# Seven block products for eight in a gated feed-forward block of an fp32 transformer kernel

## The reference, cut to what matters

```
D_MODEL = 1024
D_FF_2 = ((8 * D_MODEL // 3 + 255) // 256) * 256
def swiglu(h, w_gu, w_down):
    a, b = jnp.split(h @ w_gu, 2, axis=-1)
    return (jax.nn.silu(a) * b) @ w_down
...
    x = x + mx[2] * (jnp.concatenate([att_x, hg_x], axis=-1) @ w_out[l])
    x = x + mx[5] * swiglu(modulate(rmsnorm(x, g_norm2[l]), mx[3], mx[4]), w_gu[l], w_down[l])
return rmsnorm(x, g_final)
```

## Time and profile before

| | |
|---|---|
| median of 3 runs | 3163.41 us (3162.6 to 3164.22) |
| span of the profiled execution | 3166.7 us (first to last instruction; the page gives no time around it) |
| PE busy | 3023.6 us, 15087 matmuls |
| DVE busy | 1568.1 us, 1932 instructions |
| ACT busy | 1077.0 us, 1601 instructions |
| POOL busy | 634.1 us, 497 instructions |

### The profile page before, as it was taken

The page is one execution under the profiler, slowest core; times in us unless marked ns, Lnnn a source line. Parts: engine busy times, 40 slices in busy tenths (PEclk is TensorE's granted clock), DMA queues, the critical chain, the costliest instruction groups (busy, mean ns, idle before and its releaser), DMA issues.

```text
span 3166.7 us, 36928 instructions
## 1 busy us (share of the span) xinstructions
PE 3023.6 (95%) x15087; PEld 2515.2 (79%) x15087; DVE 1568.1 (50%) x1932; ACT 1077.0 (34%) x1601; POOL 634.1 (20%) x497
## 2 busy tenths in 40 slices
PE   7899999989999999999988999999999999999997
PEld 5688888878788888888866778888777888888886
DVE  7566665663465544333457874556644222232224
ACT  5555555552311212221436773223323111111111
POOL 4333333321000001000407783133300000000001
PEclk9999999999999999999999999999999999999999
DMA  3111111112234332111210001101131111111111
GB/s 125 41 47 47 47 47 48 47 67 94 67 116 123 118 114 68 47 53 48 100 35 13 11 9 56 34 27 41 47 113 40 47 53 47 47 47 47 53 41 60
DMA packets 77384, 184.80 MB, mean 58 GB/s; under 512 B 7072, under 2 KB 29088, under 8 KB 77216
## 3 DMA queue, kind: packets, MB, share of 16 engines
q1 hardware_dynamic: 77216, 182.44, 18.4%
HBM read 163.87 MB, written 15.79 MB: 57 GB/s over the span
## 4 chain that ended last, share of the span: by engine, by line
PE 84%; DVE 9%; ACT 4%; issue 2%; POOL 1%; DMA 0%; POOLq 0%; SPq 0%; DVEq 0%; ACTq 0%
PE ps L520 40%; PE ps L1638 18%; PE ps L3068 8%; DVE b L3016 2%; PE ps L2541 2%; PE ps L917 1%; DVE b L509 1%; PE ps L2348 1%; PE ps L2347 1%; PE ps L2319 1%; PE ps L924 1%; PE ps L2362 1%; ACT b L501 1%; DVE b L2411 1%; PE ps L90 1%
## 5 line engine op out<-in xcount | busy, mean ns | idle before, releaser
L520 PE MATMUL ps<-b 128*128 128x512 f32 x6012 | 1486.4, 398 | 29.7 <-DVE b L509 14.8
L520 PEld LDWEIGHTS ps<-b 128*128 128x128 f32 x6012 | 1105.7, 190 | 241.3 <-issue 20.3
L1638 PE MATMUL ps<-b 128*128 128x512 f32 x2592 | 599.1, 392 | 0.7 <-DVE b L1806 0.7
L1638 PEld LDWEIGHTS ps<-b 128*128 128x128 f32 x2592 | 485.0, 187 | 109.3 <-DVE b L1806 1.1
L509 DVE TENSOR_TENSOR b<-b 128x1024 fp32r<-128x1024 f32 (+1 forms) x206 | 255.3, 1241 | 287.2 <-ACT b L501 278.5
L501 ACT ACTIVATE b<-b 128x1024 fp32r<-128x1024 f32 (+1 forms) x206 | 214.9, 1045 | 529.3 <-PE ps L1638 427.4
L3068 PE MATMUL ps<-b 128*128 128x512 f32 (+1 forms) x1464 | 325.2, 377 | 6.3 <-ACT b L3127 5.9
L3068 PEld LDWEIGHTS ps<-b 128*128 128x128 f32 x1464 | 253.1, 190 | 55.0 <-issue 10.7
L1418 POOL TENSOR_TENSOR b<-b 128x1024 f32<-128x1024 f32 x18 | 43.1, 2397 | 910.1 <-ACT b L1449 909.6
L2390 POOL TENSOR_TENSOR b<-b 128x512 fp32r<-128x512 f32 x144 | 183.4, 1298 | 46.9 <-PE ps L2348 24.7
L1822 DVE TENSOR_TENSOR b<-b,ps 128x1024 f32<-128x1024 f32 x64 | 78.1, 1220 | 152.0 <-PE ps L1638 151.9
(11 more groups left out here) (319 smaller groups left out, 3680.9 us busy)
## 6 DMA issues: line engine op xcount, KB each, us to landing
b<-in_down SPq DMA_DIRECT2D x52, 512.0 KB, 3.6
b<-in_mod SPq DMA_DIRECT2D x96, 256.0 KB, 2.7
b<-in_gu SPq DMA_DIRECT2D x44, 512.0 KB, 3.6
b<-scratch SPq DMA_DIRECT2D x38, 512.0 KB, 4.4
b<-in_dn_in SPq DMA_DIRECT2D x32, 512.0 KB, 4.9
b<-in_up SPq DMA_DIRECT2D x32, 512.0 KB, 3.8
b<-in_win SPq DMA_DIRECT2D x26, 512.0 KB, 3.7
scratch<-b SPq DMA_DIRECT2D x18, 512.0 KB, 2.9
```

The source lines that it names most:

```text
L520: ins = e.matmul(ps[:, c], w, h[:, k, c], start=first and k == 0 and i == 0, stop=last and k == KT - 1 and i == 2)
L1638: ins = e.matmul(ps[:, c], w, u[:, at[k], c], start=k == 0 and p == 0, stop=k == n - 1 and p == 2)
```

## The change

The products of the second feed-forward block are made in Strassen's form (Winograd's variant: seven products of half-size blocks and fifteen additions). The first stage (`v` = 0 to 21) is one product of eight feature tiles in, two inner tiles out, 1024 tokens: the blocks are four feature tiles, one inner tile, 512 tokens. Even `v` is the gate of an inner pair, odd `v` the value. Each of the seven steps `i` of a `v` is 12 matmuls of 128x512 (L2985), and the weights of a step are a block or a sum of blocks:

- POOL makes the sums of weight blocks S1 to S4 (128x512), ACT rounds each of the seven (`act_wide_high`), DVE takes the remainder (`dve_wide_low`, L3061), six steps ahead of PE. Every `v` has two raw tiles of 128x1024.
- The seven activation operands `xs[0..6]` (128x4x512, high and remainder) are made once at the start, from `x2`, which is stored to DRAM first: DVE normalises (`z`, L3197), POOL forms differences (`operand`), ACT rounds, DVE takes remainders (`low`, L3206, L3208).
- ACT copies three of the partial sums out of PSUM, and `dve_wide_join` adds them to the others (L3274, L3276), silu on ACT, product on DVE (L3279, L3282). POOL forms four differences of each inner pair's blocks (`hidden`), and SP stores seven tiles of 128x512 for each pair to DRAM.

The second stage (`v` = 22 to 33, called t = 0 to 11) takes inner pairs in groups of 2, 2, 1, 2, 2, 2 (`GROUPS2`), two t for each group. SP loads the seven stored tiles of a group (`hidden` in `sp_wide`) into four buffers, ACT rounds them, DVE takes the remainder (`low_hidden`, L3162) into the seven or eight slots that are now `xs[3..6]`, and PE runs seven steps of 12 matmuls (6 for the group of one pair) with L3027. DVE adds each step's two banks to `w.x`, which was loaded again from DRAM (L3249). The end follows as before, with the last squares in halves.

The core of the diff:

```diff
-    units += mlp("gu", "down2", FF2, 6, True)
+GROUPS2 = ((0, 1), (2, 3), (10,), (4, 5), (6, 7), (8, 9))
+class Wide:
...
+        first = [(v, i) for i in range(5) for v in range(2)] + [(v, i) for v in range(2) for i in (5, 6)]
+        self.steps = first + [(v, i) for v in range(2, len(self.width)) for i in range(7)]
...
+    def t_after(self, v, i):
+        if v == self.na - 1 and i >= 3:
+            return [2 * (i - 3), 2 * (i - 3) + 1]
+        t = v - self.na
+        if t > 0 and t % 2 and 7 * (t // 2) + i + 8 < self.n_t():
+            return [7 * (t // 2) + i + 8]
+        return []
...
+    def wide_memory(self):
...
+        w.xs = [put(four + 16384 * i, [128, 4, 1024], F32R) for i in range(3)]
+        w.xs += [b[:, 4 * i:4 * i + 4, :] for b in (self.b_hi, self.b_lo) for i in range(2)]
...
+        w.ts = [put(four + 32768 + 4096 * i, [128, 2, 512]) for i in range(4)]
+        w.x = put(four, [128, KT, T])
...
+    def sp_wide(self, e, w):
...
+        def hidden(n):
...
+            if n < 4:
+                e.wait_ge(*P.at("st", w.na - 1, 2))
+            else:
+                e.wait_ge(*V.at("tlo", n - 4))
...
+            if v <= w.na and v % 2 == 0 and v:
+                store(v // 2 - 1)
+            if v + 2 < len(w.width):
+                load(v + 2)
+            if v == w.na - 1:
+                for k in range(KT):
+                    if k % 4 == 0:
+                        e.wait_ge(*P.at("st", v, k // 4))
...
+                    e.dma_start(w.x[:, k, :], self.scratch[2][:, k, :]).then_inc(*self.xl[k].up("x2"))
...
+    def pe_wide(self, e, w):
...
+                if i == 6:
+                    e.wait_ge(*V.at("q22", v))
...
+            if i in (2, 3, 4, 6):
+                e.wait_ge(*V.at("ad", t, {2: 0, 3: 1, 4: 2, 6: 4}[i]))
...
+    def dve_wide(self, e, w):
...
+            if i >= 3:
+                self.dve_wide_join(e, w, v, i)
+            self.dve_wide_low(e, w, s + 6)
+            if v == w.na - 1:
+                for n in w.t_after(v, i):
+                    self.low_hidden(e, w, n, V)
+        for s in range(w.index[w.na, 0], len(w.steps)):
...
+            e.wait_ge(*P.at("st", v, i))
...
+            for j in range(2):
...
+                ins = e.scalar_tensor_tensor(out=x, in0=self.wide_half(t, (0, 1, 0, 1, 0, 2, 0)[i], j), scalar=mod[:, 40 + n, 0:1],
+                                             in1=x, op0=ALU.mult, op1=ALU.add)
+            ins.then_inc(*V.up("ad", t, i))
+            self.dve_wide_low(e, w, s + 6)
+            for n in w.t_after(v, i):
+                self.low_hidden(e, w, n, V)
...
+    def pool_wide(self, e, w):
...
+        for v in range(1, n_u):
+            if v + 1 < n_u:
+                s1(v + 1)
+                s3(v + 1)
+            for i in range(7):
+                if i == 1 and v % 2 == 0 and v <= w.na:
+                    hidden(v // 2 - 1)
+                if v + 1 < n_u and i in (2, 3):
+                    (s2, s4)[i - 2](v + 1)
```

More of the change, by code:

```diff
@@ L128, in unit_list, with mlp @@
     units += [("dn_out", m, 1024) for m in range(8)]
-    def mlp(up, down, n_ff, ring, gated):
-        first = [0, n_ff] if gated else [0, 1]
+    def mlp(up, down, n_ff, ring):
+        first = [0, 1]
         out = [(up, i, 1024) for i in first]
@@ L135, in mlp @@
             if kind == "up":
-                out += [(up, i, 1024) for i in ([f, n_ff + f] if gated else [f]) if i not in first]
+                out += [(up, f, 1024)] if f not in first else []
             else:
@@ L325, with __init__, tile, quad @@
 PIECES = (slice(TC, TC + 512), slice(TC + 512, TA), slice(0, TC))
+GROUPS2 = ((0, 1), (2, 3), (10,), (4, 5), (6, 7), (8, 9))
+class Wide:
+    def __init__(self, name, j0, n_ff, groups):
+        self.name, self.j0, self.groups = name, j0, groups
+        self.na = n_ff
+        self.down = [(g, q) for g in range(len(groups)) for q in range(2)]
+        self.width = [512] * self.na + [256 * len(groups[g]) for g, q in self.down]
+        first = [(v, i) for i in range(5) for v in range(2)] + [(v, i) for v in range(2) for i in (5, 6)]
+        self.steps = first + [(v, i) for v in range(2, len(self.width)) for i in range(7)]
+        self.index = {step: s for s, step in enumerate(self.steps)}
+        order = [p for pairs in groups for p in pairs]
+        self.place = {p: n for n, p in enumerate(order)}
+    def tile(self, v, c):
+        return self.raw[(2 * v + c) % 4]
+    def quad(self, v, name):
+        w = self.width[v]
+        b = self.tile(v, 0 if name[0] == "1" else 1)
+        return b[:, 0:w] if name[1] == "1" else b[:, w:2 * w]
+    def weight(self, v, i):
+        t = self.temp[v % 2][:, 0:self.width[v]]
+        return (self.quad(v, "11"), t, t, t, self.quad(v, "21"), self.quad(v, "12"), self.quad(v, "22"))[i]
+    def n_t(self):
+        return 7 * len(self.groups)
+    def t_step(self, n):
+        g, i = divmod(n, 7)
+        return self.na + 2 * g + 1, i
+    def t_after(self, v, i):
[5 more added lines that the diff above has]
+        return []
+    def t_slot(self, n):
+        r = n % 8
+        b = self.xs[3 + r // 2]
+        return b[:, 2 * (r % 2):2 * (r % 2) + len(self.groups[n // 7]), :]
 def with_context(u):
@@ L448, in memory @@
         self.x2 = sb([128, KT, T], side="right")
-        with ExitStack() as ph:
-            self.m2 = {"sq": [sb([128, T], ctx=ph) for _ in range(2)], "acc": sb([128, T], ctx=ph), "x": self.x2}
-            self.m2["uhi"], self.m2["ulo"] = (sb([128, 6, T], F32R, ph) for _ in range(2))
+        self.wide_memory()
         flat = self.iv[0].rearrange("p a b -> p (a b)")
@@ L461, in signals @@
         self.wl = [new(f"weights{i}_loaded", 16) for i in range(RAW)]
+        self.wlx = new("weights_extra_loaded", 16)
+        self.ust, self.tl = new("hidden_stored", 16), [new(f"hidden{i}_loaded", 16) for i in range(4)]
         self.wh, self.ww = new("weights_high"), new("weights_low")
@@ L1499, in dve_project @@
             x, ps = m["x"][:, i, :], self.psl[i % 3]
-            if gate is not None:
-                e.wait_ge(*P.at("rf"))
-                e.scalar_tensor_tensor(out=x, in0=x, scalar=self.par("norm_final")[:, i:i + 1], in1=self.psl[3],
-                                       op0=ALU.mult, op1=ALU.mult).then_inc(*V.up("first", i))
-                e.wait_ge(*V.last())
-            elif i == KT - 1:
+            if i == KT - 1:
                 for k in range(KT - 1):
@@ new lines, in act_wide_high @@
+    def act_wide_high(self, e, w, s):
+        P, A, V, G = self.mm2
+        if s >= len(w.steps):
+            return
+        v, i = w.steps[s]
+        if s < 6:
+            e.wait_ge(*self.gm.at(w.j0 - SPL + s // 2))
+        else:
+            e.wait_ge(*P.at("st", *w.steps[s - 6]))
+        if i in (0, 5):
+            e.wait_ge(*self.wide_source(w, v, 0).at("w", v, 0))
+        elif i == 6:
+            e.wait_ge(*self.wide_source(w, v, 1).at("w", v, 1))
+        else:
+            e.wait_ge(*G.at({1: "S1", 2: "S2", 3: "S4", 4: "S3"}[i], v))
+        e.activation(self.wide_slot(w, s)[0], w.weight(v, i), ACT.Copy).then_inc(*A.up("whi", s))
@@ L2837, in sync_program @@
         self.sp_gla(e)
[L2838 to L2839 removed]
+        self.sp_wide(e, self.w2)
         self.sp_last(e)
@@ L3176, in down_tiles, with seven_tiles @@
     return np.concatenate(out)
+def seven_tiles(w, groups):
+    out = []
+    for pairs in groups:
+        for q in range(2):
+            for odd in range(2):
+                tile = np.zeros((128, 1024), w.dtype)
+                at = 0
+                for f_odd in range(2):
+                    for j in range(2):
+                        for p in pairs:
+                            f, n = 2 * p + f_odd, 4 * q + 2 * j + odd
+                            tile[:, at:at + 128] = w[128 * f:128 * f + 128, 128 * n:128 * n + 128]
+                            at += 128
+                out.append(tile)
+    return np.stack(out)
 def cols_of(v):
```

510 lines of the change are left out of this document (464 added, 46 removed).

## The result

The changed kernel takes 3151.08 us in the median (3149.71 to 3151.77, five runs), the kernel before in the same session 3163.41 (3162.0 to 3168.62). The ratio is 0.996, with a 95% interval of 0.9947 to 0.9972. The gain is 12 us where 46 were forecast; 3151.1 lies 34 us above the predicted time and one above the upper end of the range. The profiled execution has a span of 3148.9 us against 3166.7, 17.8 less. Why is told at the end.)

The account below looks back on a forecast made before the run. PE, never waiting in the stage, was taken as the bound. Terms −97.3 + 10.3 + 2 + 15 + 26 − 2 = −46.0 gave a span of 3120.7, so 3117 us as median, range 3092 to 3150.

Parts of the forecast that it names:

- What PE saves, −97.3: Second feed-forward block: 2772 matmuls remain of 3168, 631.0 us against 728.3, with +2.6 for operands 0 to 2.
- The start, +10.3: v = 0 and 1: PE waits for operands, +9.2 with slow clock, less 1.9, plus 3 for POOL and DVE contention.
- The −1.9 ahead of it: Just ahead of the block's first matmul: the remainder PE waits for has 512 columns and comes earlier, −1.9 us.
- The first stage in its stride, +2: v = 2 to 21: work of DVE, ACT and POOL is hidden behind PE; +2 us (0 to 11).
- a sign that it is wrong: Prediction wrong if PE waits in v = 2 to 20, 128x512 remainders average well above 0.7, or crossing idle leaves 5 to 25.
- The crossing, +15: From v = 21 to t = 0: late hidden tiles hold DVE, PE waits 8.4 and 4.0, slow clock 2.6; +15 us.
- The second stage, +26: t = 0 to 11: 3.6 at t = 1, 7, 9, 13.9 at t = 4 and 5, 8.5 for POOL's sums; +26 us.
- The end, −2: After the last add: squares in halves make POOL's last sum ready earlier, where PE waited 2.10 us; −2 us.
- POOL against DVE: Odd t of the second stage: SBUF instructions of POOL and DVE hold one another, 8.5 us, counted in the second stage.
- The second rival: All through the stage POOL and DVE exclude one another, 196 POOL instructions holding PE 0.4 us each: 3184, slower; chance 0.10.
- The first: Rival: PE is fed nearly everywhere; only 13.9 of t = 4 and 5, 5 and 6 stay: about 3089; chance 0.10.
- The third: Rival: second stage waits on DVE in even t too, +3 for each t, and 25 at the crossing: about 3150; chance 0.13.

Follow-up runs that it names:

- experiments 1 and 2: First: changed kernel plus an unused 32 byte tile in the first block, 3139.68 us. Second: kernel before with `cw` as a view of `lbw`, 3174.82 us.
- experiment 7: Changed kernel with single weight blocks in the second stage, so POOL makes no weight sums there (output not the reference's): 3139.35 us, ratio 0.9923.
- experiment 6: Changed kernel without POOL's 16 operand differences at the start (output not the reference's): 3139.47 us, ratio 0.992.

## Why the prediction was wrong, step by step

**What PE saves, −97.3.** The count is right (the 384 matmuls that it calls an up step are four of them, which changes no pace). The pace of operands 0 to 2, "792 matmuls between the two paces; I take the middle, +2.6", was mis-sized: 8.43 us for 36 is 234 ns, so the term is 792 × 7.5 ns = +5.9, 3.3 more, of which 2.8 fall in the long stretch. The step's reasoning "the slower pace belongs to the tiles" pointed at the cause, a tile's place, and stopped there.

**The step that is missing.** No term had the first block. The diff changed where its tiles lie, and its 1536 matmuls went from 226.7 to 233 ns (9.8 us by the timeline, 11.4 and 10.9 by experiments 1 and 2). The earlier trace rows had shown both paces for the same instruction, and the rule I drew from them was never asked of the tiles that the diff moves.

**The clock behind each wait.** The prediction priced slow matmuls at two places, 2.6 at the start and 2.6 at the crossing, and at none in the second stage. In the changed kernel 27 matmuls of the start, 13 of the crossing and 36 of the second stage begin while the granted clock is 0.50 (1.2 GHz), at about 0.43 us each instead of 0.227: 5.4, 2.6 and 7.2 us. That is 15 for the 5.2 in the sum, so 10 of the 34 missing microseconds. They lie inside the rows of the table and are not to be added to them. In the second stage they followed the waits of 4.64 and 5.08 and two of the three of 2.22, so a wait that is priced by its length alone is priced too low here.

**The start, +10.3.** Measured 11.0 more. The failed sentence is "and 3 more for POOL and DVE in each other's way", and with it the price of POOL's differences, "1.1 to 1.3": they take 1.58 beside DVE, and DVE's remainders 1.11. The queue was also read one item short: the sum of v = 1, step 4, stands behind operand 2 on POOL. The waits came to 15.0 for a forecast of 9.6 (12.2 less the 2.6 of slow clock), the slow matmuls to 5.4 for 2.6. Without the differences the stretch took 49.9, beside queues that ended at 47.3 with them: so the rest of that count was short too, by at least 2.6. The −1.9 ahead of it was right: from the start of L90 to the first block matmul it is 7.71 us against 9.94.

**The first stage in its stride, +2.** Right in size and place. The prediction called the wait for `q22` ahead of step 6 the tightest, and it is the one that shows. Timeline of v = 3, POOL, DVE and the weight loads of step 6:

```profile
2513.74 1.29 POOL L3293 TENSOR_TENSOR b<-b 128x512 f32<-128x512 f32 x1
2513.84 1.74 DVE L3279 TENSOR_TENSOR b<-b,b 128x512 f32<-128x512 f32 x1
...
2515.70 2.61 PEld L2985 LDWEIGHTS ps<-b 128*128 128x128 f32 x12 [0.39 <-DVE b L3279]
```

DVE's product takes 1.74 us beside POOL, where it takes 0.69 alone, and PE's weight load stands 0.39 for it. This comes again in each of the nine odd v from 3 to 19 and costs 0.28 each, 2.5 in all. With 720 × 7.5 ns = 5.4 of pace that is all but 0.4 of what the 1668 matmuls take beyond 378.1. The hidden load cost no more than this, though a remainder took 0.86 on average instead of 0.68: DVE is busy for 190.50 of 386.36 us, half the time. (The prediction had named remainders well above 0.7 as a sign that it is wrong; they were, and in this stage it hardly mattered.)

**The crossing, +15.** Right in mechanism and place, 3.7 short. It has one gap before step 6, released by DVE, of 11.05 instead of 8.4, since the first hidden tile landed at T + 19.7 and not at T + 17.1; then a granted clock of 0.50 and a second wait of 4.64 for the forecast 4.0. In that second wait two pairs of wide remainders take 4.54 and 3.42 us, where the first two pairs take 2.50 and 2.36. What runs beside them on POOL is not weight sums but the four differences of the last hidden pair:

```profile
2881.43 7.75 POOL L3357 TENSOR_TENSOR b<-b,b 128x512 f32<-128x512 f32 x4 [14.79 <-DVE b L3279]
```

In experiment 7, without weight sums, these pairs take 4.53 and 3.43. A kernel without the four differences wasn't run.

**The second stage, +26.** Measured 30.6: 14.7 in t = 4 and 5 (forecast 13.9), three waits of 2.22, 6.7 (forecast 3.6), and 9.2 in the rest (forecast 8.5 for POOL's sums). The sum is near, but in part by luck: of the 30.6 some 7 are slow matmuls, for which there was no term. The split between DVE's load and POOL isn't right either: without POOL's sums 11.7 us go, and the 2.22 with them.

**The end, −2.** It didn't come: PE waits 2.51 us for POOL's last sum, in the earlier trace rows 2.10.

**POOL against DVE.** This is the step that ran through several terms, +3, +8.5 and the rival with 0.10. Groups of the changed kernel between 2479 and 2860 us, then of the second stage, then the second stage of experiment 7:

```profile
L3061 DVE TENSOR_TENSOR b<-b,b 128x512 fp32r<-128x512 f32 x78 | 67.2, 862 | 79.8 <-ACT b L3053 79.8
L3279 DVE TENSOR_TENSOR b<-b,b 128x512 f32<-128x512 f32 x27 | 28.1, 1042 | 2.8
L3276 DVE TENSOR_TENSOR b<-b,ps 128x512 f32<-128x512 f32 x27 | 18.5, 684 | 13.8 <-PE ps L2985 13.8
```

```profile
L3061 DVE TENSOR_TENSOR b<-b,b 128x512 fp32r<-128x512 f32 x37 | 31.8, 859 | 3.0 <-ACT b L3053 2.4
```

```profile
L3063 DVE TENSOR_TENSOR b<-b 128x512 fp32r<-128x512 f32 x49 | 35.2, 719 | 0.0
```

Instructions with both inputs in SBUF went from 681 ns alone to 860 and 1042, the joins with one input from PSUM stayed at 684. The Trainium skill ("SBUF — State Buffer", Who interferes with whom) says just this of the two kinds, and the trace agrees. The second rival, that it holds PE "all through the stage", is refuted: in the first stage DVE has room for most of it and PE loses 2.5 us. Its price comes where DVE or POOL has no room: 11.6 us at the start (experiment 6) and 11.7 in the second stage (experiment 7), 23 for which I had 11.5. Both numbers hold POOL's queue and the slow matmuls behind the waits as well, so the contention alone is less.

**The other rivals.** The first, 3089 with PE fed nearly everywhere, is refuted by the 15.0 us of waits at the start and 15.7 at the crossing. The third had about 3150, within 1.1 us of what was measured, but that is luck: its mechanism, DVE holding PE in every even t, isn't in the trace: behind the crossing and outside the group of one pair, the even t have two waits, of 0.60 and 0.62.

**Sum.** 9.8 ahead of the stage, 11.0, 3.7, 3.7 and 4.6 in it and 2.0 behind it are 34.8, for the 34.1 between 3117 and 3151.1. The terms that failed are thus the first block, at nothing for 9.8, the start, +10.3 for 21, and the clock behind each wait, 5.2 for 15, which is spread over the start and the second stage.

## What to carry to other kernels

When a diff removes, adds or aliases a tile, ask which tiles move in memory with it, and what pace the matmuls that read them had at their old place: 32 bytes were worth 11 us here, in a block that the diff doesn't touch. When work goes to POOL beside DVE, price both engines' instructions with two SBUF inputs from rows where both run, and count the queue to its last entry; here it cost 2.5 us of 386 where DVE is half idle, and 11 to 12 each at the start of the stage and where DVE is full. Price a wait together with the slow matmuls behind it, from rows where that happened. Before forecasting a saving, look at the stretches where the new queue fills and drains: here the start and the crossing alone took over 40 of the 97 us that the seven products saved.
